# A two-layer hybrid step: the next layer's first modulation columns are made behind this layer's convolution, and the first projection weights wait for the first gathered rows

## The reference, cut to what matters

```python
mod = (jax.nn.silu(c) @ lp['w_mod'] + lp['b_mod']).reshape(-1, N_MOD, D_MODEL)   # c or c_ctx
h = rmsnorm(x, lp['norm1_g']) * (1 + mod[:, 1, None]) + mod[:, 0, None]
mix, ctx_out = mixing_sublayer(h, lp, ctx)       # four branches, gates sigmoid(h @ w_gate + b_gate)
x = x + mod[:, 2, None] * mix
h = rmsnorm(x, lp['norm2_g']) * (1 + mod[:, 4, None]) + mod[:, 3, None]
x = x + mod[:, 5, None] * hier_moe(h, lp)        # two experts of sixteen per row
```

## Time and profile before

| | us |
|---|---|
| median of 3 runs | 2786.13 (2786.0 to 2787.79) |
| the profiled execution | 2792.74 |
| its span | 2791.2 |
| TensorE busy | 2248.3 (81%) |
| VectorE busy | 1388.4 (50%) |
| ScalarE busy | 995.0 (36%) |
| GpSimd busy | 228.9 (8%) |
| mean granted clock of TensorE | 0.885 of full speed |

### The profile page before, as it was taken

One profiled execution on the slowest core, in us unless ns is written; L12 is line 12 of the kernel. 1 busy time (PEld: TensorE's weight loads), 2 busy tenths in 40 slices (PEclk: granted clock), 3 DMA queues, 4 the chain that ended last, 5 costly groups with the idle time before them and its releaser, 6 DMA issues.

```text
span 2791.2 us, 50199 instructions
## 1 busy us (share of the span) xinstructions
PE 2248.3 (81%) x20372; PEld 1899.2 (68%) x20372; DVE 1388.4 (50%) x1773; ACT 995.0 (36%) x1448; POOL 228.9 (8%) x251
## 2 busy tenths in 40 slices
PE   4998698898888975989459896888888799588980
PEld 2787688787774764777248785877878658467760
DVE  2225834434346544888242275344343373458873
ACT  3113234222220133777241323432232102257771
POOL 0002111101110001000100031111011000200001
PEclk9998899989898977999769998999898799589995
DMA  7114322323226307999722242233233252279986
GB/s 316 61 61 129 99 84 91 104 85 100 92 88 233 141 36 271 396 392 397 282 85 91 86 136 73 74 112 104 88 105 93 104 210 91 113 294 396 398 333 248
DMA packets 102282, 466.89 MB, mean 167 GB/s; under 512 B 12160, under 2 KB 28800, under 8 KB 75008
## 3 DMA queue, kind: packets, MB, share of 16 engines
q1 hardware_dynamic: 81792, 352.36, 34.8%
q0 software_dynamic: 10320, 75.91, 7.3%
q10 hardware_dynamic: 9936, 35.35, 3.1%
HBM read 389.64 MB, written 94.90 MB: 174 GB/s over the span
## 4 chain that ended last, share of the span: by engine, by line
PE 55%; issue 19%; DVE 9%; DMA 6%; ACT 6%; POOL 4%; SPq 0%; DVEq 0%; ACTq 0%; POOLq 0%
PE ps L870 53%; ACT we_hi L1629 3%; PE ps L873 3%; DVE we_lo L2223 2%; POOL wg_lo L763 2%; DMA x_kept<-x 1%; DMA arena<-in_experts 1%; DMA arena<-expert_out,slots 1%; POOL expert_rows L844 1%; DMA expert_out<-rows 1%; DVE arena L2253 1%; DMA rests_last<-hz_lo 1%; DMA arena<-expert_rows 0%; DVE arena L1989 0%; POOL arena L811 0%
## 5 line engine op out<-in xcount | busy, mean ns | idle before, releaser
L2223 DVE TENSOR_TENSOR we_lo<-arena,we_hi 128x2048 fp32r<-128x2048 f32 x150 | 339.3, 2289 | 92.5 <-ACT we_hi L1629 92.5
L870 PE MATMUL ps<-hz_hi,wg_hi 128*128 128x320 f32 x1024 | 349.6, 341 | 24.6 <-DMA rests_last<-hz_lo 19.0
L870 PE MATMUL ps<-arena 32*32 32x32 f32 (+5 forms) x7408 | 295.6, 225 | 53.7 <-DVE arena L1989 14.2
L870 PE MATMUL ps<-hz_hi,wg_lo 128*128 128x320 f32 x1024 | 330.9, 323 | 0.0
L870 PEld LDWEIGHTS ps<-arena 32*32 32x32 f32 (+4 forms) x7408 | 206.8, 120 | 146.7 <-issue 143.7
L1629 ACT CAST we_hi<-arena 128x2048 fp32r<-128x2048 f32 x150 | 282.9, 1912 | 3.2 <-DMA arena<-in_experts 2.9
L873 PE MATMUL ps<-fix,arena 128*128 128x128 f32 x836 | 133.8, 305 | 164.3 <-DMA arena<-expert_rows 65.9
L870 PE MATMUL ps<-rests,wg_hi 128*128 128x320 f32 x768 | 249.8, 325 | 0.0
L873 PEld LDWEIGHTS ps<-fix,arena 128*128 128x128 f32 x836 | 107.8, 156 | 189.1 <-DMA arena<-expert_rows 66.1
L870 PEld LDWEIGHTS ps<-hz_hi,wg_hi 128*128 128x128 f32 x1024 | 204.7, 200 | 39.3 <-issue 22.0
L870 PEld LDWEIGHTS ps<-hz_hi,wg_lo 128*128 128x128 f32 x1024 | 205.9, 201 | 0.0
(11 more groups left out here) (309 smaller groups left out, 4040.0 us busy)
## 6 DMA issues: line engine op xcount, KB each, us to landing
arena<-in_experts SPq DMA_DIRECT2D x150, 1024.0 KB, 8.9
ring<-in_stream SPq DMA_DIRECT2D x26, 2048.0 KB, 8.4
ring<-in_gate_stream SPq DMA_DIRECT2D x64, 512.0 KB, 3.9
arena<-in_mod_stream SPq DMA_DIRECT2D x128, 256.0 KB, 3.1
expert_rows<-in_stream POOLq DMA_DIRECT2D x50, 512.0 KB, 5.6
arena<-expert_rows SPq DMA_DIRECT2D x50, 512.0 KB, 7.1
expert_out<-rows ACTq DMA_DIRECT2D x50, 512.0 KB, 8.2
gates<-arena SPq DMA_DIRECT2D x128, 160.0 KB, 2.6
```

The lines of the kernel that those rows point to most:

```text
L870: return nc.tensor.matmul(out, lhsT, rhs, start=start, stop=stop)
L2223: V.tensor_tensor(we_lo[n % RAW], raw[n % RAW], we_hi[n % HIS].bitcast(F32), ALU.subtract).then_inc(piece_split, 1)
```

## The change

The first four modulation vectors of the first layer are made ahead of the loop, from an array of their own (`first_mod`). Those of the next layer are made during this layer's convolution, as 16 pieces of 128 columns (`NEXT` = 16): SP loads a piece of 512 KB (`load_next`, two buffers), TensorE makes its strip products behind one gate part each, from part 14 to part 29, ScalarE copies the row, TensorE turns it into columns two pieces later, and at the end one copy takes all 16 to mod_cols. The bias is added by one VectorE operation at the head of the layer. In the last layer the pieces are zeros and their result isn't used. So the loop's head no longer loads, multiplies, copies or turns modulation weights; ScalarE's root of the norm in the first layer now stands behind the modulation copies in its list. At the end of a layer the two ring loads, now of `w_in`, wait for the first two gathers. Several semaphores that were used once in a layer are merged; their waits are the same.

```diff
+FIRST_SLOTS = 4
+NEXT = FIRST_SLOTS * 4
+NEXT_FROM = closed(LN_AT) - NEXT
...
+        next_w = [arena[:, at:at + KT * P].rearrange("p (k c) -> p k c", k=KT) for at in (16000, 16000 + KT * P)]
+        next_rows = [arena[:, at:at + P] for at in range(16000 + 2 * KT * P, 16000 + 2 * KT * P + 4 * P, P)]
...
 SP
+            for i in range(FIRST_SLOTS):
+                if i >= RING:
+                    sp.wait_ge(mod_mm, i - RING + 1)
+                sp.dma_start(ring[:, (i % RING) * SLOT:(i % RING + 1) * SLOT], a["first_mod"][i]).then_inc(slot_loaded[i % RING], 16)
             for u in range(RING):
+                sp.wait_ge(mod_mm, FIRST_SLOTS - RING + u + 1)
                 load(u).then_inc(slot_loaded[u], 16)
...
-                for _ in range(SLOTS_MOD):
-                    sp.wait_ge(mod_mm, now.next("mod_mm"))
-                    load(u).then_inc(slot_loaded[u % RING], 16)
-                    u += 1
...
+                def load_next(e):
+                    src = a["next_mod"][bass.ds(now.layer * NEXT + e, 1)].rearrange("o p (k c) -> (o p) k c", k=KT)
+                    sp.dma_start(next_w[e % 2], src).then_inc(next_loaded[e % 2], 16)
...
                     sp.wait_ge(sig_done, now.next("sig_done", 2))
                     at = i % 8 * HALF
                     sp.dma_start(gates_dram[i // 8, :, at:at + HALF], stage[:, i % STAGES]).then_inc(gates_kept[i % STAGES], 16)
+                    for e in range(2 * i - NEXT_FROM, 2 * i - NEXT_FROM + 2):
+                        if -2 <= e < NEXT - 2:
+                            if e >= 0:
+                                sp.wait_ge(next_mm, now.value("next_mm", e + 1))
+                            load_next(e + 2)
...
                 sp.wait_ge(down_mm, now.value("down_mm", 2 * TILES))
                 sp.sem_inc(waits_settled, 1)
+                sp.wait_ge(rows_back[0], now.value("rows_back", 32))
+                sp.sem_inc(waits_settled, 1)
                 for _ in range(RING):
                     load(u).then_inc(slot_loaded[u % RING], 16)
...
 TensorE
+            for i in range(FIRST_SLOTS):
+                pe.wait_ge(slot_loaded[i % RING], 16 * (i // RING + 1))
+                strip_products(4 + i, 512, slot(i)).then_inc(mod_mm, 1)
+            pe.wait_ge(constants_loaded, 3 * 16)
+            for i in range(FIRST_SLOTS):
+                mod_columns(i, 4 + i)
+            pe.wait_ge(next_done, 1)
             with pe.Fori(0, DEPTH) as layer:
-                for i in range(SLOTS_MOD):
-                    pe.wait_ge(slot_loaded[i % RING], now.load(i))
-                    mod_rows_products(i, i, 4 + i, range(KT)).then_inc(mod_mm, 1)
-                pe.wait_ge(constants_loaded, 3 * 16)
-                for i in range(SLOTS_MOD):
-                    mod_columns(i, 4 + i)
-                pe.wait_ge(modc_done, now.value("modc_done", SLOTS_MOD))
                 h_transposes()
...
-                behind(closed(CONV_AT), closed(LN_AT))
-                pe.wait_ge(conv_done, now.next("conv_done"))
+                for n in range(closed(CONV_AT), closed(LN_AT)):
+                    behind(n, n + 1)
+                    e = n - NEXT_FROM
+                    if e >= 0:
+                        if e == 0:
+                            pe.wait_ge(cin_done, now.next("cin_done"))
+                        if e >= 4:
+                            pe.wait_ge(next_row, now.value("next_row", e - 3))
+                        pe.wait_ge(next_loaded[e % 2], now.value("next_loaded", 16 * (e // 2 + 1)))
+                        strip_products(e % 4, P, next_w[e % 2]).then_inc(next_mm, 1)
+                        if e >= 2:
+                            next_columns(e - 2)
+                next_columns(NEXT - 2)
+                next_columns(NEXT - 1)
+                pe.wait_ge(conv_rope_done, now.value("conv_rope_done", 1))
...
 ScalarE
+            for i in range(FIRST_SLOTS):
+                mod_row_out(i, 4 + i)
+            for i in range(FIRST_SLOTS):
+                ins = mod_column_out(i, 4 + i)
+            ins.then_inc(next_done, 1)
             with act.Fori(0, DEPTH) as layer:
                 root(rstd)
                 act.wait_ge(params_loaded, now.next("params_loaded", 32))
-                for i in range(SLOTS_MOD):
-                    mod_row_out(i, 4 + i)
-                for i in range(SLOTS_MOD):
-                    mod_column_out(i, 4 + i)
...
-                behind_out(closed(CONV_AT), closed(LN_AT))
+                for n in range(closed(CONV_AT), closed(LN_AT)):
+                    behind_out(n, n + 1)
+                    e = n - NEXT_FROM
+                    if e >= 0:
+                        act.wait_ge(next_mm, now.value("next_mm", e + 1))
+                        if e >= 4:
+                            act.wait_ge(nextT_mm, now.value("nextT_mm", e - 3))
+                        nc.scalar.copy(next_rows[e % 4], bank(e % 4, P)).then_inc(next_row, 1)
+                act.wait_ge(nextT_mm, now.value("nextT_mm", NEXT))
+                nc.scalar.copy(modc[:, 0:NEXT, :], bank(5, 2 * NEXT).rearrange("p (j g) -> p j g", g=2)).then_inc(next_done, 1)
...
 VectorE
                 x_scaled()
-                dve.wait_ge(modc_done, now.next("modc_done", SLOTS_MOD))
+                dve.wait_ge(next_done, now.value("next_done", 0))
+                V.tensor_tensor(modc[:, 0:NEXT, :], modc[:, 0:NEXT, :], over(col("bmod")[:, 0:NEXT], 2, 2), ALU.add).then_inc(dve_chain, 1)
+                dve.wait_ge(dve_chain, now.next("dve_chain"))
                 mod_scale(KT, "norm1")
```

More of the change, by code:

```diff
@@ L265, in build @@
         final_done = sem("final_done")
-        g_mm = sem("g_mm")
         gate_mm = sem("gate_mm")
@@ L298, in build @@
         nl_ready = sem("nl_ready")
-        oA_done = sem("oA_done")
+        next_done = sem("next_done")
+        next_loaded = [sem(f"next{i}_loaded") for i in range(2)]
+        next_mm = sem("next_mm")
+        next_row = sem("next_row")
+        nextT_mm = sem("nextT_mm")
         oB_done = sem("oB_done")
@@ L995, in _ @@
                 behind(0, closed(CONV_AT))
-                pe.wait_ge(vn_done, now.next("vn_done"))
+                pe.wait_ge(first_done, now.value("first_done", 1))
                 wsT = col("wsT").rearrange("p (g t) -> p g t", g=4)
@@ L1431, in mod_row_out @@
             def mod_row_out(i, bk):
-                act.wait_ge(mod_mm, now.value("mod_mm", i + 1))
+                act.wait_ge(mod_mm, i + 1)
                 nc.scalar.copy(mod_row[i], bank(bk)).then_inc(mod_rows, 1)
             def mod_column_out(i, bk):
-                act.wait_ge(modT_mm, now.value("modT_mm", i + 1))
-                for j in range(4 * i, 4 * i + 4):
-                    ins = A(modc[:, j, :], bank(bk)[:, 2 * (j - 4 * i):2 * (j - 4 * i) + 2], ACT.Identity, bias=col("bmod")[:, j:j + 1])
-                ins.then_inc(modc_done, 1)
+                act.wait_ge(modT_mm, i + 1)
+                return nc.scalar.copy(modc[:, 4 * i:4 * i + 4, :], bank(bk, 8).rearrange("p (j g) -> p j g", g=2))
             def round_chunk(q):
@@ L1531, in _ @@
                 branch_out(1)
-                act.wait_ge(qkT_mm, now.next("qkT_mm"))
+                act.wait_ge(branch_mm, now.value("branch_mm", 2))
                 act.wait_ge(keys_ready, now.next("keys_ready"))
@@ L2086, in _ @@
                 dve.wait_ge(dve_chain, now.next("dve_chain"))
-                dve.wait_ge(g_mm, now.next("g_mm"))
+                dve.wait_ge(branch_mm, now.value("branch_mm", 4))
                 V.tensor_tensor(y, y, ps[:, 0:NB * W].rearrange("p (b c) -> p b c", b=NB), ALU.mult).then_inc(oC_done, 1)
@@ L2403 @@
     arrays = {
-        "stream": stream, "gate_stream": gate, "mod_stream": behind, "wbranch": wbranch, "experts": np.concatenate([up, down], 2),
+        "stream": stream, "gate_stream": gate, "mod_stream": behind, "first_mod": mod[0, :FIRST_SLOTS], "next_mod": after, "wbranch": wbranch, "experts": np.concatenate([up, down], 2),
         "cols": np.concatenate([np.concatenate([cols[n].reshape(L, P, COLS[n][1]) for n in COLS], 2), np.zeros((1, P, NCOLS), np.float32)]),
```

105 lines of the change are left out of this document (55 added, 50 removed).

## The result

| kernel | median, us | against the kernel before, 95% interval |
|---|---|---|
| before | 2786.74 (2786.0 to 2787.79, 4 runs) | |
| changed | 2833.55 (2821.44 to 2857.02, 4 runs) | 1.0178 [1.0107, 1.0249] |
| changed, again, on another chip | 2829.34 (2810.28 to 2867.4, 9 runs; before there 2794.12, 26 runs) | 1.0097 [1.0061, 1.0133] |

The change made the kernel slower by some 1 to 2%, 33 to 47 us. Three of the nine runs of the repeat, and three of the 26 beside it, were in a slower state of the chip; the ratios, and the 33, go by the fast runs alone (medians 2825.24 and 2792.63). The forecast had said slower too, but its 2792 was 42 us too low and its range ended at 2807. The profiled execution took 2826.15 us, its span 2824.6: 33.4 more than the profiled execution of before.

A forecast was written before the change was run, and what follows sets the result against it. It took the chain of waits as the bound: VectorE in the convolution, DMA at the seam. Terms 31.6 - 19.7 - 5.9 - 1.8 + 1.3 = +5.5 gave 2798.2 profiled, 2792 on the median; 8-in-10 range 2779 to 2807.

The forecast's parts named there:

- convolution, layer one: Convolution: TensorE waits for late pieces and reaches the transposes 16.8 us late, less 1.0 for its clock; loss 15.8 us.
- convolution, layer two: Convolution of the second layer: the same loss of 15.8 us, 31.6 in all for both layers.
- seam: Between the layers, last store to last block of x: store lands sooner, gathers start earlier; gain 19.7 us.
- behind the seam: Last block to first projection product: modulation rows and columns no longer stand before the transposes; gain 5.9 us.
- end of layer two: Last store lands 8.3 us earlier, but two loads run beside the gathers, 26.5 instead of 20.0; gain 1.8 us.
- start: Kernel's start: ScalarE's root stands behind the modulation columns, first scaling at 58.4 instead of 57.11; loss 1.3 us.
- its own sign: Test the prediction set itself: wrong if the convolution stage grew by over 28 us.
- The rival of loads in time: Convolution: SP asks a unit earlier, TensorE's 13.4 us fit into the 16.1, no cost; 2760 us, chance 0.10.
- the unit of 8.0 us: Convolution: a gate unit with two pieces and the wait takes 8.0 us on average instead of 4.0 to 4.2.
- The clock: Convolution: stalls halve TensorE's clock, a unit takes 9.8 us; 8 more a layer if half meet it; 2808, chance 0.11.
- The rival by which the gathers keep pace: Both layer ends: first pair to last block takes 20.0 us despite the loads; -6.8, 2779 us, chance 0.12.
- the 28 that the forecast gives for the rule: Seam, first pair to last block: by one packet per queue in turn, some 28 us instead of 26.5.

The follow-up runs named there:

- the run with the earlier loads: Changed kernel, but SP asks for piece e+2 once piece e's products are done, ahead of the next gate chunk and the gates' store: 2786.21 us, ratio 0.9984.
- all repairs together: Changed kernel with earlier piece loads, ring loads waiting for eight gathers, and first two pieces asked for behind unit 5's store: 2763.91 us, ratio 0.9894.
- the filling: Changed kernel with the gate chunk asked for behind the pieces, plus 14 overwritten products ahead of each second piece's wait: 2824.49 us; without these products 2841.72.
- eight gathers: Changed kernel with earlier piece loads, and the two ring loads waiting for the first eight gathers instead of two: 2771.05 us, ratio 0.9929.

## Why the prediction was wrong

Its terms, in the profiled execution:

| term | forecast | measured | from |
|---|---|---|---|
| convolution, layer one | +15.8 | +30.7 | first layer-norm row, 328.18 to 358.91 |
| convolution, layer two | +15.8 | +28.1 | the same, from the first projection product: 254.6 to 282.8 |
| seam | -19.7 | -13.8 | store to last block, 56.9 to 43.1 |
| behind the seam | -5.9 | -6.0 | last block to first product, 33.6 to 27.5 |
| end of layer two | -1.8 | +1.2 | store to last block, 38.7 to 39.9 |
| start | +1.3 | -0.1 | first product, 72.73 to 72.63 |
| sum | +5.5 | +40.1 | |

The unchanged stretches gave this profile 9.0 back (-15.7 and +6.7); 31 of the profiles' 33.4 are accounted for, and the two medians, 47 and 33 us above before, lie on both sides of 40.

**The mechanism was right.** SP asks too late, TensorE stands eight times a layer, VectorE waits for it: this was the forecast, and two runs that only load earlier, or not again, take it away. By its own sign, a convolution longer by over 28 us, the forecast was wrong in both layers: 30.7 and 28.1. The rival of loads in time (2760) had its condition in the run with the earlier loads, and that took 2786, since the seam gave less than forecast. That all repairs together come to 2764 is luck and doesn't bear its price out.

**The term that failed is the unit of 8.0 us.** From the head of unit 7, where the unit before it ends, to the transposes the forecast had 66.0 us (276.56 to 342.6); it took 82.0, from 275.57. Of the 16.0 that are missing, 9.0 are the clock (with the filling against without), 4.6 the chunk's place in the queue, for which I had 0.4 in each second unit, and 2.4 the rest; in layer two 13.3 are missing, and these parts are 8.0, 1.9 and 3.4. The chunk's part is the least sure of them, since the two profiles of the changed kernel differ as much here: 79.3 to 83.6 us. The filled kernel without the clock's fall needed 68.5 and 69.3, so the sum of products, landing and stand was itself sound to within 2.5 and 3.3 us.

**The clock was a rival and not the forecast.** I gave it 0.11, at 8 us a layer if half the units met it, because a gap of 2.5 us had kept the full clock in the scan. That row was a poor neighbour: it showed one gap, not one in each unit. The fall came behind most of the stands and cost 8.0 to 9.0 a layer. That this is near the rival's price is luck: the work of a unit was 5.7 us by the forecast's own terms (0.43, twice 1.79, twice 0.84), which doubles to 11.4 and not to its 9.8, so half the units would have cost 14 a layer. The Trainium skill (TensorE: Matmul & The Clock Gate, "HAM oscillation") says that a matmul loop that waits for a DMA in each turn can be throttled anew each turn. This trace agrees: from 294 on stretches of 1.00 and 0.66 in turn, one pair for each stand. The error was to make the two exclude each other: the rival took the stand to go when the clock fell, but the next load is asked for only behind the slower part, so that the stand stayed at 2.6 in the mean and the clock came on top.

**The seam.** The store landed in 5.0, not 2.7; first gather to first pair was 6.8, as forecast. From first pair to last block I had 26.5, and it was 30.0: the sum left out 3.7 MB that ScalarE and GpSimd move there in both kernels. Its own steps also fall short: 14.9 and 3.5 make 18.4, not the 20.5 that it goes on with, and no row gives the 2.1 between. The rival by which the gathers keep pace (20.0; its terms add up to -7.5, not -6.8) was wrong for this wait and right for a later one (19.9 behind eight gathers).

The Trainium skill (DMA: Bandwidth & Descriptors, "Queues, rings and completion order") says that each engine takes one packet from each queue in turn. I had set that aside because the earlier trace rows gave q0 461 packets to q1's 292, and that was a misreading: the count takes in times in which one queue moved next to nothing (1366 to 1369: 58 packets of q1 and none of q0; 1378 to 1381: 26 and 279). Between them, from 1372 to 1378, q1 had 143 packets and q0 140. In the changed kernel, while the projection loads ran, from 1388 to 1399 (packets, MB, share of 16 engines):

```profile
q1 hardware_dynamic: 210, 3.18, 69.8%
q0 software_dynamic: 205, 0.74, 16.9%
q10 hardware_dynamic: 166, 0.61, 13.6%
```

The trace agrees with the rule: q1 and q0 have even counts, and of their bytes q0 has 19%. Taking the rule would not have mended the sum, since another order of the packets changes none of the bytes, and bytes are what it lacked; the 28 that the forecast gives for the rule doesn't come out of its steps either.

**The start** cost nothing: the modulation copies came at 44.4 to 47.8 and not at 50.2, so what stands behind the root was done before x's copy to DRAM, for which VectorE and ScalarE waited in both kernels (first scaling at 57.02, before at 57.11).

**The range** was too narrow because its far case, the clock, was priced alone, and because the spread of a run (46 us on one chip, before the change) doesn't show in three runs that agree within 1.8.

## What to carry to other kernels

A load whose issue stands behind a store, whose store waits for the work before it, is a closed loop: its period is landing plus all work between landing and issue, whatever slack the engine has. Ask at the place where the buffer comes free. When TensorE stands once in each turn of such a loop, price the half clock behind the stand as well as the stand, not instead of it; and when transfers are moved into another window, sum all the bytes of that window, those of engines that weren't touched too. Read the shares of two queues only from a stretch in which both move data throughout.

## What was not expected of the hardware

VectorE's convolution got faster, 62.69 us instead of the 67.29 of the earlier trace rows, with the same 60 operations. The line in the kernel before (durations in ns, min/median/max), and GpSimd's splits of the gate weights beside it:

```profile
L1840 DVE SCALAR_TENSOR_TENSOR x<-x,cols x60: 887/900/3124, 258.4 to 324.8; 128x655 f32<-128x655 f32 x60
```

```profile
L763 POOL TENSOR_TENSOR wg_lo<-ring,wg_hi x7: 2337/2406/2430, 261.7 to 311.4; 128x1024 fp32r<-128x1024 f32 x7
```

An operation takes 0.9 us, but up to 3.1: some of them are longer by about the length of a split. Seven splits stood beside the 60 in the kernel before; in the changed one TensorE's late units put two of them behind the end. The twelve profiles have 24 convolutions, and in each there are as many operations above 1 us as splits beside them (one split that starts in the last 0.4 us not counted): with seven the 60 operations take 67.1 to 67.3 us, with six 64.7 to 65.0, with five 62.7 to 62.9 and with four 60.6 to 60.7. So each further split adds some 2.2 us, most of its own 2.3 to 3.0. That a split holds VectorE up was read from these traces and not tried by itself.
